# Both heads of an attention item turned in one visit, with the second in a borrowed bank, and the items laid on fewer steps

## What is computed

```python
def dilated_mixer(h, w_in, w_out):
    B, S, _ = h.shape
    proj = (h @ w_in).reshape(B, S, N_GROUPS, 3, N_HEADS, HEAD_DIM)
    pos = jnp.arange(S, dtype=jnp.float32)
    outs, lses = [], []
    for g, (window, dil) in enumerate(DILATED_PATTERNS):
        q = partial_rotary(proj[:, :, g, 0], pos)
        k = partial_rotary(proj[:, :, g, 1], pos)
        v = proj[:, :, g, 2]
        o, lse = dilated_band_attention(q, k, v, dil, window // dil)
        outs.append(o)
        lses.append(lse)
    wts = jax.nn.softmax(jnp.stack(lses, axis=0), axis=0)
    o = jnp.einsum('gbsh,gbshd->bshd', wts, jnp.stack(outs, axis=0))
    return o.reshape(B, S, ATTN_WIDTH).astype(h.dtype) @ w_out
```

## Time and profile before

| | before |
| --- | --- |
| median of 3 runs | 2173.26 us (2173.2 to 2175.18) |
| time of the profiled execution | 2173.4 us |
| its span, first to last instruction | 2171.3 us |
| PE busy in the span | 2160.9 us, 100% |
| DVE, ACT, POOL busy | 1222.6, 857.6, 437.7 us |
| mean granted TensorE clock | 1.000 |
| span of phases 1 to 5 (79.2 to 504.6 us) | 425.4 us |

### The profile page before, as it was taken

One profiled execution on the slowest core, in us unless ns is written; L12 is line 12 of the kernel. 1 busy time (PEld: TensorE's weight loads), 2 busy tenths in 40 slices (PEclk: granted clock), 3 DMA queues, 4 the chain that ended last, 5 costly groups with the idle time before them and its releaser, 6 DMA issues.

```text
span 2171.3 us, 27585 instructions
## 1 busy us (share of the span) xinstructions
PE 2160.9 (100%) x10792; PEld 1773.8 (82%) x10792; DVE 1222.6 (56%) x2106; ACT 857.6 (39%) x1455; POOL 437.7 (20%) x307
## 2 busy tenths in 40 slices
PE   9999999999999999999999999999999999999998
PEld 7788887888888888887777888888887888888887
DVE  5655557667644443266567544423698966555443
ACT  5334324436333232234444323222469564434432
POOL 3532233352401010133335101002300001110100
PEclk9999999999999999999999999999999999999999
DMA  5222223222233333332222233333333332322322
GB/s 172 78 69 78 82 79 118 83 69 76 90 97 97 97 97 97 97 117 88 79 78 86 91 97 97 98 97 97 97 102 112 98 102 88 93 77 82 94 78 88
DMA packets 87902, 201.51 MB, mean 93 GB/s; under 512 B 7736, under 2 KB 46904, under 8 KB 87776
## 3 DMA queue, kind: packets, MB, share of 16 engines
q1 hardware_dynamic: 83184, 189.62, 28.3%
q10 hardware_dynamic: 4592, 10.13, 1.5%
HBM read 197.54 MB, written 2.18 MB: 92 GB/s over the span
## 4 chain that ended last, share of the span: by engine, by line
PE 93%; DVE 4%; ACT 1%; issue 1%; POOL 1%; DMA 0%; SPq 0%; ACTq 0%; DVEq 0%; POOLq 0%
PE PS L630 52%; PE PS L696 6%; PE PS L698 5%; PE PS L697 5%; PE PS L721 2%; PE PS L722 2%; PE PS L723 2%; PE PS L779 1%; PE PS L769 1%; PE PS L793 1%; PE PS L1042 1%; PE PS L1030 1%; PE PS L1019 1%; PE PS L1106 1%; DVE WL L2076 1%
## 5 line engine op out<-in xcount | busy, mean ns | idle before, releaser
L2076 DVE TENSOR_TENSOR WL<-WR,WH 128x1024 fp32r<-128x1024 f32 x353 | 460.6, 1315 | 657.8 <-ACT WH L1356 657.3
L1356 ACT ACTIVATE WH<-WR 128x1024 fp32r<-128x1024 f32 x353 | 368.9, 1057 | 561.3 <-DMA WR<-in_ws 544.8
L630 PE MATMUL PS<-XH,WH 128*128 128x512 f32 x1040 | 406.9, 391 | 0.0
L630 PE MATMUL PS<-XL,WH 128*128 128x512 f32 x1040 | 404.7, 389 | 0.0
L630 PE MATMUL PS<-XH,WL 128*128 128x512 f32 x1040 | 404.7, 389 | 0.0
L630 PEld LDWEIGHTS PS<-XH,WH 128*128 128x128 f32 x1040 | 195.2, 188 | 43.0 <-issue 2.6
L630 PEld LDWEIGHTS PS<-XH,WL 128*128 128x128 f32 x1040 | 195.2, 188 | 40.7
L630 PEld LDWEIGHTS PS<-XL,WH 128*128 128x128 f32 x1040 | 195.3, 188 | 40.6 <-issue 0.7
L696 PE MATMUL PS<-XH,WH 128*128 128x512 f32 x544 | 220.7, 406 | 0.0
L698 PE MATMUL PS<-XH,WL 128*128 128x512 f32 x544 | 212.9, 391 | 0.0
L697 PE MATMUL PS<-XL,WH 128*128 128x512 f32 x544 | 212.1, 390 | 0.0
(11 more groups left out here) (388 smaller groups left out, 3795.1 us busy)
## 6 DMA issues: line engine op xcount, KB each, us to landing
WR<-in_ws SPq DMA_DIRECT2D x281, 512.0 KB, 3.5
WR<-in_ws SPq DMA_DIRECT2D x144, 256.0 KB, 3.3
B_CB<-gates ACTq DMA_DIRECT2D x8, 512.0 KB, 4.1
A_WB<-weight_rows_out ACTq DMA_DIRECT2D x24, 128.0 KB, 3.2
XTOK<-in_x SPq DMA_DIRECT2D x4, 512.0 KB, 5.9
out<-OUT SPq DMA_DIRECT2D x8, 256.0 KB, 2.0
R_D<-in_decay ACTq DMA_DIRECT2D x4, 256.0 KB, 2.6
GAIN<-in_post ACTq DMA_DIRECT2D x1, 512.0 KB, 4.9
```

Source lines behind the costliest of these rows:

```text
L630: mm = pe.matmul(PS[:, bank + o, :], l, r, start=first and kk == 0 and i == 0, stop=last and kk == 1 and i == 2)
L1356: nc.scalar.activation(WH[:, s, :], WR[:, s, :], ACT.Copy).then_inc(hi_ready, 1)
L2076: tt(WL[:, s, :], WR[:, s, :], WH[:, s, :].bitcast(F32), ALU.subtract).then_inc(lo_ready, 1)
```

## The change

The function `scored` and its calls are replaced by tables that name for each item the step of its scores, of its head 0 and of its head 1. Where both heads stand in the same step, the pair is a twin: the second head is transposed into a bank of the projection (`turned_bank`) which the present quarter does not write, bank 2 during an even quarter and bank 0 during an odd one. PE then no longer waits for the copy of head 0 between the two; it waits until the bank's last contents have been read (`rot_sh`, or `v_ready` in quarter 0), and the next quarter, which writes that bank, first waits for both copies (`pt_copied`, `TWIN_LAST`). There are 19 twins: four in each of phases 1, 2, 3 and 5 (at steps 2, 6, 10, 14 in phase 1, and 2, 5, 9, 13 in the others) and three in phase 4 (steps 5, 9, 13). The other items keep their heads in neighbouring steps and in bank 6. The last body's items, which stand in phases 5 and 6, are not moved.

```diff
--- before.py
+++ after.py
@@ -324,25 +324,34 @@
                 spot = (phase, first + i * (last + 1 - first) // len(ticks))
                 SPOT.setdefault(spot, []).extend(entries)
 
-        def scored(m):
-
-            count, ticks = len(ITEMS_A[A_BODIES[m][1]]), []
-            for i in range(count + 2):
-                ticks.append([entry for entry, there in (
-                    (("scores", m, i), i < count), (("values", m, i - 2), i >= 2),
-                    (("turned", m, i - 1, 0), 1 <= i <= count)) if there])
-                ticks.append([("turned", m, i - 1, 1)] if 1 <= i <= count else [])
-            return [t for t in ticks if t]
-
-        place(1, scored(0), 0, 20)
-        place(2, scored(1), 0, 20)
-        place(3, scored(2), 0, 17)
+        def scored(phase, m, steps):
+
+            for i, (scores, first, second) in enumerate(steps):
+                entries = [(scores, ("scores", m, i))] if scores is not None else []
+                if i >= 2:
+                    entries.append((scores if scores is not None else first, ("values", m, i - 2)))
+                if first is not None:
+                    entries += [(first, ("turned", m, i - 1, 0)), (second, ("turned", m, i - 1, 1))]
+                for step, entry in entries:
+                    SPOT.setdefault((phase, step), []).append(entry)
+        FEW = [(0, None, None), (2, 2, 2), (5, 5, 5), (9, 9, 9), (None, 13, 13)]
+        MANY = [(0, None, None), (2, 2, 2), (4, 4, 5), (6, 6, 6), (8, 8, 9), (10, 10, 10), (12, 12, 13), (14, 14, 14),
+                (None, 16, 17)]
+        LATER = [(3, None, None), (5, 5, 5), (7, 7, 8), (9, 9, 9), (11, 11, 12), (13, 13, 13), (15, 15, 16), (17, 17, 18),
+                 (None, 19, 20)]
+
+        def all_values(phase, m, steps, last):
+            scored(phase, m, steps)
+            SPOT.setdefault((phase, last), []).append(("values", m, len(steps) - 2))
+        all_values(1, 0, MANY, 18)
+        all_values(2, 1, FEW, 15)
+        all_values(3, 2, FEW, 15)
         place(3, [[("stats", 0), ("weights", 0)], [("turn", 0)]], 19, 22)
         first = [("merge", 0, t, j) for t in range(4) for j in range(3)]
         place(4, [[("fetch", k) for k in range(3)]], 0, 0)
         place(4, [[first[k]] + ([("fetch", k + 2)] if 1 <= k < 10 else []) for k in range(12)], 1, 23)
-        place(4, scored(3), 4, 21)
-        place(5, scored(4), 0, 14)
+        all_values(4, 3, LATER, 21)
+        all_values(5, 4, FEW, 15)
         def last(kind, *rest):
             return (kind, 5) + rest
 
@@ -361,6 +370,17 @@
             for entry in entries:
                 SPOT[spot].append(len(ENTRIES))
                 ENTRIES.append(entry)
+
+        TWIN, TWIN_LAST = {}, {}
+        for (phase, step), found in SPOT.items():
+            for e in found:
+                if ENTRIES[e][0] == "turned" and ENTRIES[e][3] == 1 and e - 1 in found and ENTRIES[e - 1] == ENTRIES[e][:3] + (0,):
+                    TWIN[e] = (phase, step // 4)
+                    TWIN_LAST[phase, step // 4 + 1] = A_ITEM0[ENTRIES[e][1]] + ENTRIES[e][2]
+
+        def turned_bank(e):
+
+            return 2 * ((TWIN[e][1] + 1) % 2) if e in TWIN else T_BANK
 
         def copies_first(e):
 
@@ -735,6 +755,8 @@
                         pe.wait_ge(v_ready, 4 * m - 2 + 2 * n)
                     elif n:
                         pe.wait_ge(r_done, DT)
+                    if (m, n) in TWIN_LAST:
+                        pe.wait_ge(pt_copied, 2 * TWIN_LAST[m, n] + 2)
                     for j in range(2):
                         yield from pair_unit(u + 2 * n + j, 4 * j, XH, XL, first_bank(m, n), j == 0, j == 1,
                                              None if m or n else x_ready(0))
@@ -744,6 +766,8 @@
                         pe.wait_ge(rot_sh, 8 * m + 8 if m else 4)
                     elif j == 0:
                         pe.wait_ge(rot_sh, 8 * m + 6 if m else 2)
+                        if (m, 4) in TWIN_LAST:
+                            pe.wait_ge(pt_copied, 2 * TWIN_LAST[m, 4] + 2)
                     mm = value_unit(u + 8 + j, j, g, half, j == 0, j == 3)
                     if half:
                         mm.then_inc(unit_used, 1)
@@ -773,10 +797,16 @@
                     _, m, i, h = ENTRIES[e]
                     pair, segs, n = item(m, i)
                     pe.wait_ge(p_ready, 2 * n + h + 1)
-                    if 2 * n + h:
+                    if e in TWIN:
+                        body, quarter = TWIN[e]
+                        if quarter:
+                            pe.wait_ge(rot_sh, 8 * body + 2 * quarter)
+                        else:
+                            pe.wait_ge(v_ready, 4 * body)
+                    elif 2 * n + h:
                         pe.wait_ge(pt_copied, 2 * n + h)
                     for c in range(0, width(segs), P):
-                        mm = pe.transpose(PS[:, T_BANK, c:c + P], A_P[:, n % 2, h, c:c + P], ident)
+                        mm = pe.transpose(PS[:, turned_bank(e), c:c + P], A_P[:, n % 2, h, c:c + P], ident)
                     mm.then_inc(t_done, 1)
                 elif kind == "values":
                     _, m, i = ENTRIES[e]
@@ -1393,7 +1423,7 @@
                     if n:
                         act.wait_ge(pv_done, n)
                     w = width(segs)
-                    nc.scalar.activation(A_PT[:, 1, 0:w], PS[:, T_BANK, 0:w], ACT.Copy).then_inc(pt_copied, 1)
+                    nc.scalar.activation(A_PT[:, 1, 0:w], PS[:, turned_bank(e), 0:w], ACT.Copy).then_inc(pt_copied, 1)
                 elif ENTRIES[e][0] == "values" and ENTRIES[e][1] == 5:
                     _, m, i = ENTRIES[e]
                     pair, segs, n = item(m, i)
```

## The result

| | before | after |
| --- | --- | --- |
| median of 4 runs of each | 2173.35 us (2173.2 to 2175.18) | 2188.14 us (2187.06 to 2189.97) |
| after / before | | 1.0068 (1.0056 to 1.008) |
| profiled execution, its span | 2173.4, 2171.3 us | 2189.0, 2186.9 us |
| phases 1 to 5, each | 90.30, 79.65, 80.04, 90.77, 84.66 us | 93.09, 81.69, 81.23, 97.67, 86.91 us |
| together | 425.4 us | 440.6 us |

The account below looks back on a forecast made before the run. PE was taken to bound the kernel, with 93% of the span. Waits of 5.6 + 2.1 + 5.5 less a gain of 1.4 made 11.8 us more, so 2185.0 us; own range 2179 to 2190, eight in ten 2178 to 2191.

Parts of the forecast that it names:

- What bounds the kernel: Phases 1 to 5 are priced in PE's time alone: work removed is gained in full, waits paid in full.
- Wait A: Next quarter waits for both copies after seven even-step twins: 0.7 us four times in phase 1, 0.95 in phases 2, 3, 5.
- Wait B: Phases 2, 3, 5, step 5: head 1 waits until DVE has turned the tile before; 0.7 us each, 2.1 together.
- Wait C: Phase 4, steps 5, 9, 13: head 1 waits for DVE's turn; 1.5, 1.8 and 2.2 us, 5.5 together.
- The clock: Sign of being wrong: granted clock falls below 1.000 after a PE gap, lengthening every matmul behind it; no size given.
- The gain: Phases 1 to 5: joined visits, fewer visits ahead of value matmuls and small waits removed save 1.4 us, at most 3.
- The spacing and the small waits: Fewer visits ahead of value matmuls (phases 1, 2; one more in 5), 0.3 us; mask and late-transposition waits gone, 0.9 us.
- Joining: Sharing one visit saves 0.01 us for each of 19 twins, 0.2 us; bounds nothing and 1.0 us.
- Steps 9 and 13 of phases 2, 3 and 5: PE stays at least 0.5 us behind DVE at these places, so no wait was counted.
- slower rival: Steps 9 and 13 of phases 2, 3, 5 wait as step 5 does, adding 4 to 9 us: 2189 to 2194; chance 0.12.
- not slower: Twins' copies done in time: Wait A and Wait B vanish, Wait C under 2 us; 2172 to 2174 us; chance 0.14.
- chain A: Even steps of Wait A: head 1's copy, ACT's high part, DVE's low part, then head 0's copy; PE released at 6.23 us (phase 1).

Follow-up runs that it names:

- both: Changed kernel with head 0 copied before the low part in seven even-step twins, and both tiles of a quarter turned at its last step: 2171.79 us.
- pool_late: Changed kernel, but POOL starts a body's first tile only when DVE has turned the second too (phases 1 to 5): 2182.33 us.
- apart_turn_early: Changed kernel without twins, head 1 one step after head 0 in bank 6, and both tiles of a quarter turned in the same step: 2172.22 us.

## Why the prediction was right, and where its sum was off

The forecast of 2185.0 us was right in direction, mechanism and place, and the 2188.14 us lie inside its range. Step by step:

- **What bounds the kernel.** Right. Every microsecond that PE waited in phases 1 to 5 is in the time, and both, which takes the waits away, gives all of it back.
- **Wait A.** 5.6 predicted, 5.7 measured, and 5.1 less in the median when its cause was removed. It could be had this exactly because each link had its row and the order on ACT and DVE decided the rest.
- **Wait B.** 2.1 predicted, 2.8 measured in the first execution and 1.6 in the second. The 0.7 each stood between three cases that I had named, and the traces show all three, each smaller than my count: 0 where DVE wins (0.15 in the count), 0.3 in phase 3, where the low part takes 1.97 us (0.9), and some 1.25 where POOL wins (1.5). The Trainium skill (SBUF — State Buffer, section Who interferes with whom) has the two kinds of operation shut each other out for a whole operation. The trace agrees in kind: the low part that began beside POOL's operation ended 1.08 us after it (195.80 against 194.72), nearly a whole operation of 1.23 us later.
- **Wait C.** 5.5 predicted, 6.1 measured. Steps 9 and 13 were sized from rows of the same steps before and came to 3.7 instead of 4.0. The mis-sized term is step 5, 1.5 against 2.40. I had no row for it and placed it under its neighbours; but with item 1's work there DVE's split and its product both meet POOL, and pool_late shows that this is 2.1 of the 2.4.
- **The clock.** Left out of the sum, though named as what would make it wrong. It cost 1.6 us in the profiled execution.
- **The gain.** 1.4 predicted, 1.0 here as a remainder, and 1.4 in the phases of both (424.0 against 425.4 us), in which a wait of 0.45 us still stands. That it came out is in part luck, since its terms were off. The spacing and the small waits were put at 1.2 and give 1.0 (424.4 us in apart_turn_early). Joining was put at 0.2 and is worth some 0.8 without that wait, near its upper bound of 1.0: by the phases a visit of its own costs PE 0.04 us and not 0.01, for the most part in the matmuls behind it, where I had not looked.
- **Steps 9 and 13 of phases 2, 3 and 5.** No wait, as the count said, so the slower rival fell. The rival "not slower" fell too: no link of chain A was quicker than its row.

In the profiled execution the sum missed by 3.8 us: clock 1.6, B 0.7, C 0.6, gain 0.4, A 0.1, and 0.4 at the start of the program. (It closes exactly because the gain was taken as the remainder.)

Outside the gain nearly all the misses point the same way (steps 9 and 13 of wait C apart, 0.3 us together), so the total was too low and is covered by the range, not by errors that cancel. Why a fall of the clock comes in one execution and not in the next stays open. Filling PE's wait with other matmuls was not tried, since no bank is free there.

## What to carry to other kernels

A second buffer that is borrowed from a neighbour brings the neighbour's release with it: write down what each borrowed bank waits for, and move that release ahead, before two pieces of work are joined. Where an engine works through a queue in order, what counts is what stands ahead of the releasing instruction, and here a copy of 0.55 us behind a weight split cost more than the joining could ever have saved. And a stall taken out of the engine that bounds the kernel may come back at the next place where it waits for the same chain, so take such stalls out together or price them together.

## What the runs showed of the hardware

- The same wait of PE of 2.21 us, in the same place of the same kernel, was followed in one execution by a granted clock of 0.50 for some seven matmuls (1.6 us lost) and in another by none. One of 2.69 us was followed by none, and one of 1.78 us in the same execution was. In all, six falls in five executions; none of the 8 executions without a wait of 2.2 us had one.
- A DVE product of two SBUF operands that normally takes 0.68 us took 2.01 beside POOL, and one of 1.23 took up to 2.60. Of 14 places where the two start within 0.03 us of each other, POOL got through first in the eight in which its start was 0.01 to 0.03 us ahead, DVE in the six in which both starts read the same; PE's wait behind it differs by 1.25 us.
- Three or four transpositions (0.339 and 0.444 us) cost in a visit of their own within 0.011 us what they cost in a shared one, as far as the visit itself goes. The ten matmul pitches behind such a visit are together some 0.03 us longer.
